# A hybrid encoder step: gate and up of both feed forwards by seven block products, with the down products spread between them

## What is computed

```python
D_MODEL = 1024; D_FF = 2816
def swiglu(x, w_gate, w_up, w_down):
    return (jax.nn.silu(x @ w_gate) * (x @ w_up)) @ w_down

def layer(x, w, past):
    x = x + 0.5 * swiglu(rms_norm(x, w['ffn1_norm']), w['ffn1_w_gate'], w['ffn1_w_up'], w['ffn1_w_down'])
    ...
    x = x + 0.5 * swiglu(rms_norm(x, w['ffn2_norm']), w['ffn2_w_gate'], w['ffn2_w_up'], w['ffn2_w_down'])
```

## Time and profile before

| | |
|---|---|
| median of 3 runs | 2968.98 us (2968.97 to 2969.11) |
| span of the profiled execution | 2968.9 us |
| PE, matmuls | 2842.8 us, 96% of the span |
| DVE | 1648.7 us, 56% |
| ACT | 847.9 us, 29% |
| POOL | 373.3 us, 13% |
| ffn1 / ffn2 | about 0 to 822 us / 2101 to 2969 us |

### The profile page before, as it was taken

How to read it: one execution, slowest core, us unless ns; L and a number is a source line. 1 busy time by engine, 2 the same in 40 slices (tenths; PEclk the granted TensorE clock), 3 DMA queues, 4 the chain that set the end, 5 groups by cost and what they waited for, 6 DMA issues and landing times. The chain is left out here.

```text
span 2968.9 us, 43643 instructions
## 1 busy us (share of the span) xinstructions
PE 2842.8 (96%) x15997; PEld 2661.3 (90%) x15997; DVE 1648.7 (56%) x2948; ACT 847.9 (29%) x1474; POOL 373.3 (13%) x495
## 2 busy tenths in 40 slices
PE   8999999999999999999989779899999999999998
PEld 7999999999989789999978668688899999999997
DVE  5444444444451378899454357677644444444445
ACT  4111111111132434554276425411321111111112
POOL 0000000000010034454130166410000000000000
PEclk9999999999999999999989899899999999999999
DMA  4111111111022112222210322442121111111111
GB/s 150 43 42 42 42 42 42 42 42 42 8 54 48 29 54 87 86 83 93 76 41 12 89 61 76 142 137 68 43 64 43 42 42 42 42 42 42 42 36 64
DMA packets 234890, 172.47 MB, mean 58 GB/s; under 512 B 45481, under 2 KB 216217, under 8 KB 234786
## 3 DMA queue, kind: packets, MB, share of 16 engines
q1 hardware_dynamic: 227634, 142.70, 16.7%
q10 hardware_dynamic: 4752, 18.94, 1.7%
q0 software_dynamic: 2400, 9.44, 0.9%
HBM read 136.51 MB, written 34.47 MB: 58 GB/s over the span
## 5 line engine op out<-in xcount | busy, mean ns | idle before, releaser
L524 DVE TENSOR_TENSOR ffn_prod<-ffn_silu,ffn_p_up 128x384 f32<-128x384 f32 x132 | 73.1, 554 | 758.8 <-ACT ffn_silu L432 758.8
L507 DVE SCALAR_TENSOR_TENSOR x<-ffn_p_down,x 128x512 f32<-128x512 f32 x738 | 474.8, 686 | 1.3 <-PE ffn_p_down L156 1.3
L156 PE MATMUL ffn_p_gate<-ffn_hT_hi,ffn_g_hi 128*128 128x384 f32 x1056 | 355.1, 336 | 2.3 <-DVE ffn_hT_lo L262 2.3
L156 PE MATMUL ffn_p_up<-ffn_hT_hi,ffn_u_hi 128*128 128x384 f32 x1056 | 353.6, 335 | 0.0
L156 PE MATMUL ffn_p_gate<-ffn_hT_lo,ffn_g_hi 128*128 128x384 f32 x1056 | 353.5, 335 | 0.0
L156 PE MATMUL ffn_p_gate<-ffn_hT_hi,ffn_g_lo 128*128 128x384 f32 x1056 | 353.4, 335 | 0.0
L156 PE MATMUL ffn_p_up<-ffn_hT_hi,ffn_u_lo 128*128 128x384 f32 x1056 | 353.0, 334 | 0.0
L156 PE MATMUL ffn_p_up<-ffn_hT_lo,ffn_u_hi 128*128 128x384 f32 x1056 | 352.8, 334 | 0.0
L432 ACT ACTIVATE ffn_silu<-ffn_p_gate 128x384 f32<-128x384 f32 x132 | 65.0, 492 | 860.5 <-PE ffn_p_up L156 860.5
L156 PE MATMUL ffn_p_down<-o_c_hi,o_t_lo 128*128 128x512 f32 x756 | 295.3, 391 | 0.0
L156 PE MATMUL ffn_p_down<-o_c_lo,o_t_hi 128*128 128x512 f32 x756 | 294.8, 390 | 0.0
(11 more groups left out here) (390 smaller groups left out, 5097.0 us busy)
## 6 DMA issues: line engine op xcount, KB each, us to landing
ffn_raw_g<-in_ffn_w_gate SPq DMA_DIRECT2D x44, 512.0 KB, 5.0
ffn_raw_u<-in_ffn_w_up SPq DMA_DIRECT2D x44, 512.0 KB, 6.1
ffn_raw_d<-in_ffn_w_down SPq DMA_DIRECT2D x44, 512.0 KB, 3.7
h_raw<-in_w_in SPq DMA_DIRECT2D x32, 512.0 KB, 3.9
projected_d<-sp_stage ACTq DMA_DIRECT2D x20, 576.0 KB, 2.8
conv_d<-sp_stage ACTq DMA_DIRECT2D x12, 576.0 KB, 3.2
dl_qkv<-conv_d SPq DMA_DIRECT2D x27, 256.0 KB, 3.8
x<-in_x_prompt SPq DMA_DIRECT2D x8, 512.0 KB, 7.2
```

Of the source, the lines that this page charges most:

```text
L156: mm = nc.tensor.matmul(out, stationary(k)[a], moving(k)[b], start=(start and at == 0 and i == 0), stop=(stop and 3 * at + i == n - 1))
L507: nc.vector.scalar_tensor_tensor(out=xs, in0=p_down[(NO * q + o) % 4][:], scalar=0.5, in1=xs, op0=ALU.mult, op1=ALU.add).then_inc(added, 1)
L524: nc.vector.tensor_tensor(prod[:, slot], silu[:, slot], p_up[slot][:, 0:TG], ALU.mult).then_inc(prod_done, 1)
```

## The change

A step's gate and up weights are seen as a matrix of four blocks: gate and up by the lower and the upper 512 channels. The input of the first two groups is seen as four blocks too: 512 channels by a group. Four products of blocks of the result, each a sum of two, are made from seven block products instead of eight, by sums and differences of the blocks (the scheme of Strassen in Winograd's form). The third group is made directly as before, in halves of 512 channels. Each of the seven products is 4 blocks x 3 matmuls of 384 columns.

- The sums of the input blocks (T1 to T4) are made once for each feed forward: ACT keeps the turned halves of tiles 0 to 5 in float32 too (`keep_block`), POOL combines them in twelve operations (`combine`), ACT casts them and DVE takes the rests (`keep_t_hi`, `keep_t_lo`, 128 x 1536 each). PE's turn into a bank now also waits for the copy of the tile before (`kept`).
- The sums of the weight blocks (s_1 to s_4, 128 x 512 each) are made in each step, one step ahead: DVE sums (`sum_1` to `sum_4`), ACT casts (`sum_high`), DVE takes the rests (`sum_rest`).
- The results are put together by DVE in additions that read PSUM: u2, u3, c22 (written to PSUM), c21 and c12. ACT keeps the first product aside (`keep_p1`).
- PE's order in a step is P1, the gate product of the third group in two halves, P2, P6, P5, P7, P4, P3 and the up product of the third group in two halves. The down products of the step before stand between these units, by the table `DOWNS_AFTER`. P2 and P3 add onto a bank in which a product lies.
- The gate weights have one buffer now, and the up weights too; the raw gate block is laid where the lo part will be, and is loaded when P2 has been made. There is one pair of buffers for the down weights and the products instead of two, the second ones hold the weight sums. The third product of a step and the down weights of that step are finished at the head of the next step on ACT and DVE.
- Step 0 makes the plain products. The last step has no down products between.

```diff
+DOWNS_AFTER = (0, 1, 2, 2, 2, 2, 2, 3, 2, 2, 0)
...
+    def keep_block(self, act, t):
+        if t >= 6:
+            return
+        for half in range(2):
+            slot = (1, 3, 0, 2)[2 * (t // 3) + half]
+            self.nc.scalar.copy(self.blocks[:, slot, :, t % 3 * P:(t % 3 + 1) * P],
+                                self.pT[(2 * t + half) % 4][:]).then_inc(self.kept, 1)
...
+        if 4 <= i < 16:
+            pe.wait_ge(self.kept, i - 3)
...
+        pool.wait_ge(self.kept, 2 * (j + 3) + 2)
+        self.nc.gpsimd.tensor_tensor(b22, b22, b12, ALU.subtract).then_inc(self.combined, 1)
+        pool.wait_ge(self.combined, 4 * j + 1)
...
-                    sp.wait_ge(gu_lo, 2 * n - 1)
-                sp.dma_start(raw_g[:], wg[:, :, bass.ts(n, P)]).then_inc(g_in, 16)
+                    sp.wait_ge(p2_made, n - 1)
+                sp.dma_start(a1_raw[:], wg[:, :, bass.ts(n, P)]).then_inc(g_in, 16)
...
+            def down_high(n, slot=0):
+                act.wait_ge(d_in, 16 * n + 16)
...
+                else:
+                    act.wait_ge(down, NO * n)
+                nc.scalar.copy(d_hi[:, slot], raw_d[:]).then_inc(dn_hi, 1)
...
+            def keep_product(n, g, temp, slot=0):
+                act.wait_ge(prod_done, NG * n + g + 1)
...
+                nc.scalar.copy(a_hi[:, slot, g * TG:(g + 1) * TG], temp[:]).then_inc(act_hi, 1)
...
+                    keep_product(n - 1, 2, td)
+                down_high(n - 1)
+                up_high(n)
+                keep_p1(n, x_bank)
+                silu_0(n, x_bank)
+                if not last:
+                    sum_high(n + 1, 1)
+                    gate_high(n + 1)
+                    sum_high(n + 1, 2)
+                    sum_high(n + 1, 3)
+                keep_product(n, 0, td, int(last))
+                silu_2(n)
+                silu_1(n)
+                keep_product(n, 1, ta, int(last))
+                if last:
+                    down_high(n, 1)
+                    keep_product(n, 2, td, 1)
+                else:
+                    sum_high(n + 1, 4)
...
+            act.wait_ge(norm.combined, 12)
+            act.wait_ge(norm.turned, 2 * NT)
+            norm.keep_t_hi(0)
+            norm.keep_t_hi(1)
+            first_silu(1)
+            sum_high(1, 1)
+            keep_product(0, 1, ta)
+            sum_high(1, 2)
+            sum_high(1, 3)
+            act.wait_ge(first_up, 2)
+            norm.keep_t_hi(2)
+            norm.keep_t_hi(3)
+            sum_high(1, 4)
+            gate_high(1)
+            first_silu(2)
+            keep_product(0, 2, tb)
+            in_steps(act, step, 1, LAST)
+            step(LAST, LAST % 2, True)
...
+            def gate_rest(n):
+                dve.wait_ge(gate_hi, n + 1)
...
+                    dve.wait_ge(s_sum[3], n)
...
+                nc.vector.tensor_tensor(a1_lo[:], raw, a1_hi[:].bitcast(F32), ALU.subtract).then_inc(gate_lo, 1)
...
+            def take_c22(n, y_bank):
+                dve.wait_ge(u3_done, n)
+                nc.vector.tensor_tensor(y_bank[:, 0:TG], tb[:], p_d[:, 0:TG], ALU.add).then_inc(c22_done, 1)
...
+            def step(n, q, last=False):
+                x_bank, y_bank = p_gu[q], p_gu[1 - q]
+                adds = (lambda outs: None) if last else (lambda outs: add_down(n - 1, 1 - q, outs))
+                if not known(n, 2):
+                    product_2(n - 1, y_bank)
+                down_rest(n - 1)
+                if not known(n, 2):
+                    keep_rest(n - 1, 2, td)
+                up_rest(n)
+                adds(range(0, 5))
+                take_u2(n, y_bank)
+                adds(range(5, 7))
+                if not last:
+                    sum_1(n + 1)
+                adds(range(7, 9))
+                take_u3(n, y_bank)
+                take_c22(n, y_bank)
+                if not last:
+                    sum_2(n + 1)
+                    sum_3(n + 1)
+                adds(range(9, 11))
+                take_c21(n, x_bank)
+                product_0(n)
+                if not last:
+                    sum_rest(n + 1, 1)
+                adds(range(11, 12))
+                keep_rest(n, 0, td, int(last))
+                adds(range(12, 14))
+                if not last:
+                    sum_rest(n + 1, 3)
+                take_c12(n)
+                if not last:
+                    sum_4(n + 1)
+                    gate_rest(n + 1)
+                product_1(n, y_bank)
+                adds(range(14, 16))
+                if not last:
+                    sum_rest(n + 1, 2)
+                keep_rest(n, 1, ta, int(last))
+                adds(range(16, 18))
+                if last:
+                    down_rest(n, 1)
+                    product_2(n, x_bank)
+                    keep_rest(n, 2, td, 1)
+                else:
...
+            sum_1(1)
+            first_product(1)
+            sum_2(1)
+            sum_3(1)
+            keep_rest(0, 1, ta)
+            sum_4(1)
+            norm.keep_t_lo(dve, 0)
+            norm.keep_t_lo(dve, 1)
+            sum_rest(1, 2)
+            gate_rest(1)
+            first_product(2)
+            sum_rest(1, 1)
+            keep_rest(0, 2, tb)
+            sum_rest(1, 3)
+            sum_rest(1, 4)
+            norm.keep_t_lo(dve, 2)
+            norm.keep_t_lo(dve, 3)
+            in_steps(dve, step, 1, LAST)
+            step(LAST, LAST % 2, True)
...
-            def step(n, q):
-                gate_and_up(n, q)
-                down_proj(n - 1, 1 - q)
...
+            def product(bank, hi, lo, slot, onto=False):
+                return three_passes(nc, bank[:, 0:TG], lambda k: (hi[:, k, :], lo[:, k, :]),
+                                    lambda k: (norm.bt_hi[:, slot, k, :], norm.bt_lo[:, slot, k, :]), range(NQ), not onto,
...
+            def step(n, q, downs=True):
+                x_bank, y_bank = p_gu[q], p_gu[1 - q]
+                first = known(n, 2)
...
+                    for _ in range(DOWNS_AFTER[unit] if downs else 0):
+                        if at == 0:
+                            pe.wait_ge(dn_lo, n)
+                        down_out(n - 1, 1 - q, at)
+                        at += 1
...
+                pe.wait_ge(gate_lo, n + 1)
+                if first:
+                    pe.wait_ge(silu_done[2], 1)
+                else:
+                    pe.wait_ge(prod_done, NG * n - 1)
+                product(x_bank, a1_hi, a1_lo, B11).then_inc(p1_made, 1)
+                some_down(0)
+                if first:
+                    pe.wait_ge(silu_done[1], 1)
+                else:
+                    pe.wait_ge(silu_done[2], n)
+                direct(p_c, a1_hi, a1_lo, 0)
+                some_down(1)
+                direct(p_c, a1_hi, a1_lo, 1).then_inc(dg_made, 1)
+                some_down(2)
+                pe.wait_ge(p1_kept, n)
+                product(x_bank, a1_hi[:, NQ:KD], a1_lo[:, NQ:KD], B21, True).then_inc(p2_made, 1)
+                some_down(3)
+                pe.wait_ge(s_rest[1], n)
+                pe.wait_ge(prod_done, NG * n)
+                if first:
+                    pe.wait_ge(norm.t_lo_ready, 2)
+                product(y_bank, *blocked(2), T2).then_inc(p6_made, 1)
+                some_down(4)
+                pe.wait_ge(s_rest[0], n)
+                if not first:
+                    pe.wait_ge(c12_done, n - 1)
+                product(p_d, *blocked(1), T1).then_inc(p5_made, 1)
+                some_down(5)
+                pe.wait_ge(s_rest[2], n)
+                pe.wait_ge(u2_done, n)
+                if first:
+                    pe.wait_ge(norm.t_lo_ready, 3)
+                product(y_bank, *blocked(3), T3).then_inc(p7_made, 1)
+                some_down(6)
+                pe.wait_ge(up_lo, n + 1)
+                pe.wait_ge(silu_done[0], n + 1)
+                if first:
+                    pe.wait_ge(norm.t_lo_ready, 4)
+                product(x_bank, a2_hi[:, NQ:KD], a2_lo[:, NQ:KD], T4).then_inc(p4_made, 1)
+                some_down(7)
+                pe.wait_ge(s_rest[3], n)
+                pe.wait_ge(c22_done, n)
+                product(p_d, *blocked(4), B22, True).then_inc(p3_made, 1)
+                some_down(8)
+                pe.wait_ge(c21_done, n)
+                direct(x_bank, a2_hi, a2_lo, 0)
+                some_down(9)
+                direct(x_bank, a2_hi, a2_lo, 1).then_inc(du_made, 1)
             if start:
```

More of the change, by code:

```diff
@@ L331, in ffn @@
-        silu, prod = s.sbuf("silu", [P, 2, TG]), s.sbuf("prod", [P, 2, TG])
-        p_gate = [s.psum(f"p_gate{i}") for i in range(2)]
-        p_up = [s.psum(f"p_up{i}") for i in range(2)]
-        p_down = [s.psum(f"p_down{i}") for i in range(4)]
-        norm = NormTurn(nc, s, x, ident, hT_hi, hT_lo, gain, [b[:].rearrange("p (k c) -> p k c", c=P) for b in p_down])
-        pending = None if start else Pending(nc, s, x, ops, 1.0, [p_gate[0], p_up[0], p_gate[1], p_up[1]])
+        p_gu = [s.psum(f"p_gu{i}") for i in range(2)]
@@ new lines, in ffn @@
```

(48 more changed lines are left out.)

399 lines of the change are left out of this document (249 added, 150 removed).

## The result

| | before | after |
|---|---|---|
| median of 4 runs | 2969.05 us | 2923.76 us (2921.68 to 2924.81) |
| after / before | | 0.9846, 95% interval 0.9832 to 0.9860 |
| span of the profiled execution | 2968.9 us | 2923.0 us |
| step in the loop (P1 to P1) | 37.26 us | 35.65 us |

What follows compares the result with a forecast made beforehand. TensorE's matmuls were taken to bound the kernel. 2968.9 us minus 87.4 for fewer matmuls, plus 19 for the starts, 0.5 for the last step and 4 for stalls gave 2905.0 us; range 2894 to 2937, about 0.85.

Steps and rivals of the forecast that it cites:

- stall at the first down product: PE waits there for the rest of the down weights; 0.1 us a step, 4 us for 40 steps.
- start of both feed forwards: Added copies, combinations, casts and waits before and in the first steps; 9.5 us each, 19 us for both.
- last step: Without down products, the chain of product_1 and down_rest ends about 0.5 us after the last half; 0.5 us once.
- What goes: In steps 1 to 21 of both feed forwards, 132 gate and up matmuls instead of 144; 87.4 us less.
- rival 4: Bank change or wait before each of 11 units costs 0.19 us and replaces the saved matmuls; no change, chance 0.02.
- The slack of 0.2 us: Before the first down product, down_rest ends near 39.15 us and PE wants it at 39.34 in the step.
- rival 1: VectorE becomes the step's bound, each step stalling 0.3 to 1.3 us; price 12 to 52 us, chance 0.28.
- rival 3: VectorE operations with waits don't overlap; stall 1.9 us a step, 2977 us in all, chance 0.05.
- P1's wait: At each feed forward's start, P1 waits 2.7 us on ScalarE's casts and VectorE's gate_rest.
- the rows at half clock: After the start's waits of 2.7 and 3 us, matmuls at 1.2 GHz lose 1 us each feed forward.
- rival 2: GpSimd's combinations end late and hold ScalarE; P1 waits about 6 us more each start, price 12 us, chance 0.07.
- The norms beside GpSimd: Three norms run beside the combinations, 1.87 instead of 1.28 us each; 0 to 1.8 us, taken as 0.5.

Runs made afterwards that it cites:

- the one block: Against the changed kernel: the 18 down products in one block behind the gate product of group three, VectorE's 18 adds in one piece; 2910.43 us, ratio 0.9796.
- the fourth rest behind: Against the changed kernel: VectorE takes the rest of the fourth weight sum behind the rest of the up weights in the next step; 2915.99 us.
- the short ones: Against the changed kernel: GpSimd's twelve combinations work on 8 of each 128 columns; 2921.01 us.

## Why the prediction was right, and where 19 us went

The sign, the range and the mechanism of the gain held. The terms, against the spans (2968.9 - 2923.0 = 45.9 us; 63.9 forecast):

| term of the sum | forecast | measured |
|---|---|---|
| 42 steps x 2.08 us fewer matmuls | -87.4 | -87.4 |
| rows further apart, 40 steps | 0 | +11.6 (0.29 each) |
| stall at the first down product, 40 steps forecast, 36 found | +4 (0.1 each) | +6.5 (0.18 each) |
| start of both feed forwards | +19 | +20.1 |
| last step | +0.5 | +0.5 |
| between the feed forwards, 1277.35 us instead of 1275.84 | 0 | +1.5 |

These add up to 47.2 us of gain; 1.3 is not accounted for, about half of it in step 1 and half in the last step of the second feed forward. I counted 40 steps for the stall, but the last step of a feed forward has no down products between, step 1 counts to the start, and step 20 has no stall; 18 of each are left. The 1.5 us lie in a stretch that the change doesn't touch; seven of the experiments' kernels have from 1272.75 to 1276.05 there.

**What goes** failed in one step, "with the same 12.30 us of down products". I divided 12.30 by 54 and took the mean for every matmul, though cutting the run changes which matmuls there are: the first nine of a run stand 0.232 apart, and after the change every one is among a run's first nine. It could be read before: in PE's timeline of the kernel before the first nine rows of a run of 54 (from 300.27 us to 302.36) take 2.09 us, 0.232 each, and the later ones, up to the next product at 312.57, are 0.227 apart:

```profile
300.27 0.40 PE L156 MATMUL ffn_p_down<-o_c_hi,o_t_hi 128*128 128x512 f32 x1
...
302.36 0.39 PE L156 MATMUL ffn_p_down<-o_c_hi,o_t_hi 128*128 128x512 f32 x1
```

My rival 4 named a change of unit as a cost, and I set it aside because "37.26 being 6 x 4.16 + 12.30": a sum that the mean makes true. That is the largest part of the miss, 11.6 us, shown by the one block (12.30 again) and by the fourth rest behind (35.47 with no wait left).

**The slack of 0.2 us** was the right place and the right chain, almost to the digit. I had product_2 0.62 us behind P1's start (35.8 against 35.18) and down_rest's end 3.97 behind it; the rows have 0.62 and 4.00. What failed is the last step, where I set the end of down_rest against the start of the first down matmul. The weight load of that matmul is due one matmul, 0.17, ahead of it, at 316.86, and down_rest ends at 316.87. A release 0.01 too late then costs far more than 0.01: the load starts 0.24 us behind it, at 317.11, and 0.2 of slack on paper becomes a stall of 0.18. In step 20 down_rest ends at 744.55, 0.07 ahead of its load, and there is no stall. In step 1, where PE had long been waiting, the load follows 0.05 behind the release (2155.66 to 2155.71). Why it takes 0.24 at this place in the loop no run shows. Of rival 1 the mechanism is true, and its price (0.3 to 1.3) was not reached. That DVE's distances are 0.47 and 0.60 held: 312.89 to 313.49 is 0.60. So rival 3 falls. The Trainium skill, page VectorE: DVE Perf Modes, section The DRAIN you can't avoid, which I named for it, also says that an operation that is not held starts earlier; the trace agrees with that part, 0.60 being less than the 0.68 listed.

**The start** was right in sum by luck. Parts of each feed forward, first and second: the third group's last matmul 2.5 and 3.3 us later than before (2.8 forecast); P1's wait 6.1 and 2.3 (2.7); the rows at half clock 2.8 and 1.5 (1); the first down product 0.2 and 1.4 (3). P1's long wait in the first is rival 2: the combinations end late, by 3.76 us as the short ones show. Where P1 waited long, ACT and DVE had caught up by the first down product, so the two waits are one: what is taken from the first comes back at the second, until the order changes.

**The norms beside GpSimd** (0.5 us each feed forward): with the full combinations three norms of 128 x 1024 took 1.48, 1.66 and 1.29 us in the first feed forward, with short ones 1.28, 1.28 and 1.29. In the second four norms beside the combinations took 2.13, 1.87, 2.40 and 2.03, 3.3 us more in all than at 1.28, so 0.5 was too little there. How much of it PE saw is not told apart from the copies. The Trainium skill, page SBUF — State Buffer, section Who interferes with whom, has them lock each other out for an instruction; what was added, up to 0.4 us in the first and up to 1.1 in the second, is less than a whole combination of 1.28 each time, but the sum in the second is near the 3 us that I had worked out by it.

The time of every listed run is 1.7 to 2.0 us above its span, where I took under 0.1; it is on both sides and moves the difference by nothing.

## What to carry to other kernels

A mean over a long run of matmuls is no price for the same matmuls in short runs: read the first rows of a run and its later rows apart before cutting it, and judge by the distance from step to step, since PE's busy share stood at 100% with 0.47 us of every step lost. A wait that is met a little late can cost much more than it is late, so leave room in front of the weight load and not only of the matmul. Work that must lie between matmuls was cheaper here in one block, with the adds of the engine that empties its banks in one piece beside it. At the start of a loop put first in each queue what is wanted first: the same work in another order was worth 16 us here, and moving one wait only showed the next.

## What the runs showed of the hardware

- Matmuls of 512 columns with a weight load each stand 0.232 apart in runs of six and nine, 4.13 / 18 = 0.229 in runs of 18, 0.2278 in runs of 54, and behind such a run the first matmuls of 384 take up to 0.03 us more in all. Why the first rows of a run are slower is open.
- After the same wait of 3.1 us PE's rows came at the 2.4 GHz level in some steps and at 1.2 GHz in others, with 1.6 us between the steps (38.7 and 40.3); after 5.9 us they stayed at 1.2 GHz for 5.9 us. After 2.15 us they came at 2.4 GHz in one kernel, and the first ten at 1.2 GHz in another.
- A weight load started 0.05 us behind the operation that it waited for in step 1, and 0.21 to 0.24 us behind it at the first down product in the hardware loop.
